# Feed-forward of a two-layer decoder in fp32r parts on one core: ten of eleven gate and up steps computed transposed, with the weights as stationary operand

## What is computed

```python
def rms_norm(x, g):
    y = xf * lax.rsqrt(jnp.mean(xf * xf, axis=-1, keepdims=True) + RMS_EPS)
    return (y * g.astype(jnp.float32)).astype(x.dtype)

def swiglu(x, w_gate_up, w_down):
    gate, up = jnp.split(x @ w_gate_up, 2, axis=-1)
    return (jax.nn.silu(gate) * up) @ w_down
...
        h = swiglu(rms_norm(x, g[2]), w_gate_up[layer], w_down[layer])
        x = x + rms_norm(h, g[3])
```

## Time and profile before

| | us |
|---|---|
| median of 3 runs | 799.78 |
| lowest, highest run | 798.93, 800.35 |
| profiled execution | 799.25 |
| its span | 797.5 |
| TensorE busy | 785.1 (98%) |
| VectorE busy | 503.6 (63%) |
| ScalarE busy | 382.7 (48%) |

### The profile page before, as it was taken

One profiled execution on the slowest core, in us unless ns is written; L12 is line 12 of the kernel. 1 busy time (PEld: TensorE's weight loads), 2 busy tenths in 40 slices (PEclk: granted clock), 3 DMA queues, 4 the chain that ended last, 5 costly groups with the idle time before them and its releaser, 6 DMA issues.

```text
span 797.5 us, 12942 instructions
## 1 busy us (share of the span) xinstructions
PE 785.1 (98%) x4795; PEld 689.8 (86%) x4795; DVE 503.6 (63%) x645; ACT 382.7 (48%) x469; POOL 59.4 (7%) x74
## 2 busy tenths in 40 slices
PE   8999999999999999998999999999999999999997
PEld 7999978888888888998999999999987888888885
DVE  5788987764655547776747557567546756555453
ACT  6675667443334335745545435445357433343331
POOL 1000002100000000311201202112002000000000
PEclk9999999999999999999999999999999999999999
DMA  8534665776455555287466455474722875555601
GB/s 230 172 114 132 218 191 171 238 254 219 160 173 195 181 191 162 52 219 205 111 180 170 126 165 152 140 196 125 245 80 73 275 273 164 171 197 179 222 21 53
DMA packets 158801, 135.45 MB, mean 170 GB/s; under 512 B 5176, under 2 KB 149168, under 8 KB 158768
## 3 DMA queue, kind: packets, MB, share of 16 engines
q1 hardware_dynamic: 157296, 130.75, 52.3%
q0 software_dynamic: 1376, 4.22, 2.4%
q10 hardware_dynamic: 96, 0.04, 0.0%
HBM read 133.91 MB, written 1.07 MB: 169 GB/s over the span
## 4 chain that ended last, share of the span: by engine, by line
PE 92%; ACT 3%; DVE 2%; DMA 1%; issue 1%; SPq 0%; DVEq 0%; POOLq 0%; ACTq 0%; POOL 0%
PE ps L1001 19%; PE ps L1003 19%; PE ps L1002 19%; PE ps L1007 8%; PE ps L1009 8%; PE ps L1008 8%; PE ps L1278 2%; PE ps L1268 2%; PE ps L1143 1%; PE ps L1247 1%; ACT xt L445 1%; DVE w_lo L642 1%; PE ps L1074 1%; PE ps L1241 1%; PE ps L1022 1%
## 5 line engine op out<-in xcount | busy, mean ns | idle before, releaser
L642 DVE TENSOR_TENSOR w_lo<-raw,w_hi 128x2048 fp32r<-128x2048 f32 (+2 forms) x146 | 280.4, 1941 | 35.8 <-ACT w_hi L414 34.3
L414 ACT ACTIVATE w_hi<-raw 128x2048 fp32r<-128x2048 f32 (+2 forms) x146 | 234.1, 1628 | 47.0 <-DMA raw<-in_w_kv_b 16.2
L1001 PE MATMUL ps<-w_hi,xt 128*128 128x512 f32 x352 | 139.4, 396 | 0.0
L1003 PE MATMUL ps<-w_hi,xt 128*128 128x512 f32 x352 | 137.3, 390 | 0.0
L1002 PE MATMUL ps<-w_lo,xt 128*128 128x512 f32 x352 | 137.1, 389 | 0.0
L537 ACT ACTIVATE work<-ps,stat 128x256 f32<-128x256 f32 x44 | 20.9, 476 | 199.9 <-PE ps L1003 199.9
L1007 PE MATMUL ps<-xt,w_hi 128*128 128x256 f32 x384 | 110.1, 287 | 1.1 <-DVE xt L650 0.7
L1008 PE MATMUL ps<-xt,w_hi 128*128 128x256 f32 x384 | 108.6, 283 | 0.0
L1009 PE MATMUL ps<-xt,w_lo 128*128 128x256 f32 x384 | 108.6, 283 | 0.0
L1001 PE MATMUL ps<-w_hi,ot 128*128 128x512 f32 x240 | 94.7, 395 | 0.0
L1003 PE MATMUL ps<-w_hi,ot 128*128 128x512 f32 x240 | 93.5, 390 | 0.0
(11 more groups left out here) (121 smaller groups left out, 1092.1 us busy)
## 6 DMA issues: line engine op xcount, KB each, us to landing
raw<-in_w_gate_up SPq DMA_DIRECT2D x88, 512.0 KB, 4.7
raw<-in_w_kv_b SPq DMA_DIRECT2D x96, 256.0 KB, 3.6
raw<-in_w_down SPq DMA_DIRECT2D x22, 1024.0 KB, 4.9
raw<-in_w_qkv_a SPq DMA_DIRECT2D x24, 512.0 KB, 4.8
raw<-in_w_q_b SPq DMA_DIRECT2D x48, 256.0 KB, 3.6
raw<-in_w_o_a SPq DMA_DIRECT2D x4, 1024.0 KB, 5.2
raw<-in_w_o_b SPq DMA_DIRECT2D x4, 1024.0 KB, 4.9
work<-in_norm_gains POOLq DMA_DIRECT2D x4, 512.0 KB, 5.2
```

What stands on the lines that cost most here:

```text
L414: act.activation(w_hi[:, s % CUT, 0:size(s)], raw[:, s % RAW, 0:size(s)], ACT.Copy).then_inc(hi_made, 1)
L642: dve.tensor_tensor(w_lo[:, c, 0:n], raw[:, s % RAW, 0:n], w_hi[:, c, 0:n].bitcast(F32), ALU.subtract).then_inc(lo_made, 1)
L1001: mm(out, xs[0], ws[0], start=start, stop=False)
L1003: return mm(out, xs[1], ws[0], start=False, stop=stop)
```

## The change

In steps 1 to 10 of each layer the gate and up products are made with the weights as stationary operand. A step has four of them: f (which 128 of the step's 256 hidden columns) and c (0 gate, 1 up), into bank 4 + 2f + c. For each of the eight row blocks a matmul takes the weights' high part as stationary operand and both parts of x, 256 + 256 tokens, as one moving row into the two halves of the bank; a second takes the low part and the high part of x (256 columns) into the first half. ScalarE copies the second half out, and VectorE adds it to the first. The result has hidden columns as partitions, so it needs no transpose; the norm's factors now lie along the free axis, so they are multiplied in from `rows`, once before the silu and once behind it. For that each layer's feed-forward part gets a diagonal, a spread into bank 7 and a copy of its own. Step 0 and the down products stay as they were, and step 0's hidden part is still transposed. The three loads, high parts and low parts per step remain.

The core of the diff (ScalarE, VectorE, TensorE). `up_part_of` and `gate_of` are like `gate_part_of`; `hidden_of` writes the high part into `ot`:

```diff
+            def gate_part_of(l, i, j, f):
+                n = wide_step(l, i)
+                act.wait_ge(cols_done, j * 6 + 3 * n + 2 * f + 1)
+                if n:
+                    act.wait_ge(gate_silu_made, j * 4 + 2 * n + f - 1)
+                act.activation(gate[:, f, :], bank(4 + 2 * f, SEQ, SEQ), ACT.Copy).then_inc(gate_part, 1)
+            def up_part_of(l, s, i, j, f):
+                n = wide_step(l, i)
+                act.wait_ge(*((cols_done, j * 6 + 3 * n + 2) if f == 0 else (w_used, j * 6 + s + 2)))
+                if n:
+                    act.wait_ge(hidden_made, j * 4 + 2 * n + f - 1)
+                act.activation(upper[:, f, :], bank(5 + 2 * f, SEQ, SEQ), ACT.Copy).then_inc(up_part, 1)
+            def gate_of(l, i, j, f):
+                n = wide_step(l, i)
+                act.wait_ge(gate_made, j * 4 + 2 * n + f + 1)
+                if n:
+                    act.wait_ge(hidden_made, j * 4 + 2 * n + f - 1)
+                act.activation(gate_silu[:, f, :], gate[:, f, :], ACT.Silu).then_inc(gate_silu_made, 1)
+            def hidden_of(l, i, j, f):
+                act.wait_ge(hidden_made, j * 4 + 2 * wide_step(l, i) + f + 1)
+                act.activation(ot[:, 0, hidden_at(i).start + f, :], hidden[:, f, :], ACT.Copy).then_inc(hidden_hi, 1)
             def swiglu_step(l, s0, i, j, units):
                 s = s0 + 3 * i - 1
-                for n, u in enumerate(units):
-                    if n < NT and i == 1:
-                        silu_of(l, s, i, j, n)
-                    hi(u, j)
-                    if n < NT and i > 1:
-                        silu_of(l, s, i, j, n)
+                if i > 1:
+                    up_part_of(l, s - 3, i - 1, j, 1)
+                hi(units[0], j)
+                if i > 1:
+                    hidden_of(l, i - 1, j, 1)
+                gate_part_of(l, i, j, 0)
+                gate_of(l, i, j, 0)
+                up_part_of(l, s, i, j, 0)
+                if len(units) > 1:
+                    hi(units[1], j)
+                hidden_of(l, i, j, 0)
+                if len(units) > 2:
+                    hi(units[2], j)
+                gate_part_of(l, i, j, 1)
+                gate_of(l, i, j, 1)
             def swiglu(l, s0, last_units):
                 for t in range(NT):
                     act.wait_ge(xrs_made, NT * (2 * l + 1) + t + 1)
-                    silu_of(l, s0, 0, 0, t)
+                    silu_of(l, s0, t)
                     if t == 0:
                         hi(s0 + 4)
                 swiglu_step(l, s0, 1, 0, range(s0 + 5, s0 + 8))
@@ -558,6 +601,8 @@
                     for i in (2, 3):
                         swiglu_step(l, s0, i, j, range(s0 + 3 * i + 2, s0 + 3 * i + 5))
                 swiglu_step(l, s0, STEPS - 1, 0, last_units)
+                up_part_of(l, s0 + 3 * STEPS - 4, STEPS - 1, 0, 1)
+                hidden_of(l, STEPS - 1, 0, 1)
...
+            def make_gate(l, i, j, f):
+                m = 2 * wide_step(l, i) + f + 1
+                dve.wait_ge(gate_part, j * 4 + m)
+                dve.tensor_tensor(gate[:, f, :], bank(4 + 2 * f, 0, SEQ), gate[:, f, :], ALU.add
+                                  ).then_inc(gate_summed, 1)
+                if i == 1 and f == 0:
+                    take_rows(2 + 2 * l, 7)
+                    cut_hidden(l)
+                dve.wait_ge(gate_summed, j * 4 + m)
+                dve.tensor_tensor(gate[:, f, :], gate[:, f, :], rows[:, :], ALU.mult).then_inc(gate_made, 1)
+            def make_hidden(l, i, j, f):
+                n = wide_step(l, i)
+                m = 2 * n + f + 1
+                dve.wait_ge(gate_silu_made, j * 4 + m)
+                dve.tensor_tensor(gate_silu[:, f, :], gate_silu[:, f, :], rows[:, :], ALU.mult).then_inc(gate_scaled, 1)
+                dve.wait_ge(up_part, j * 4 + m)
+                dve.tensor_tensor(upper[:, f, :], bank(5 + 2 * f, 0, SEQ), upper[:, f, :], ALU.add
+                                  ).then_inc(up_summed, 1)
+                dve.wait_ge(gate_scaled, j * 4 + m)
+                dve.wait_ge(up_summed, j * 4 + m)
+                if n:
+                    dve.wait_ge(hidden_cut, j * 4 + m - 2)
+                dve.tensor_tensor(hidden[:, f, :], upper[:, f, :], gate_silu[:, f, :], ALU.mult
+                                  ).then_inc(hidden_made, 1)
+            def lo_hidden(l, i, j, f):
+                k = hidden_at(i).start + f
+                dve.wait_ge(hidden_hi, j * 4 + 2 * wide_step(l, i) + f + 1)
+                dve.tensor_tensor(ot[:, 1, k, :], hidden[:, f, :], ot[:, 0, k, :].bitcast(F32), ALU.subtract
+                                  ).then_inc(hidden_cut, 1)
             def swiglu_step(l, i, j, units):
                 if i > 1:
-                    lo(units[0], j)
-                cut_hidden(l, i - 1, j)
-                gated(l, i, j, 0)
-                if i == 1:
-                    lo(units[0])
+                    make_hidden(l, i - 1, j, 1)
+                    lo_hidden(l, i - 1, j, 1)
+                make_gate(l, i, j, 0)
+                lo(units[0], j)
+                make_hidden(l, i, j, 0)
                 if len(units) > 1:
                     lo(units[1], j)
-                gated(l, i, j, 1)
+                lo_hidden(l, i, j, 0)
                 if len(units) > 2:
                     lo(units[2], j)
+                make_gate(l, i, j, 1)
             def swiglu(l, s0, last_units):
-                gated(l, 0, 0, 0)
+                gated(l, 0)
+                make_diagonal(2 * l + 1)
                 lo(s0 + 3)
-                gated(l, 0, 0, 1)
+                gated(l, 1)
                 lo(s0 + 4)
                 swiglu_step(l, 1, 0, range(s0 + 5, s0 + 8))
                 with dve.Fori(0, (STEPS - 3) // 2) as j:
                     for i in (2, 3):
                         swiglu_step(l, i, j, range(s0 + 3 * i + 2, s0 + 3 * i + 5))
                 swiglu_step(l, STEPS - 1, 0, last_units)
+                make_hidden(l, STEPS - 1, 0, 1)
+                lo_hidden(l, STEPS - 1, 0, 1)
...
+            def up_wide(l, s, i, j, f, c):
+                n, b = wide_step(l, i), 4 + 2 * f + c
+                if i == 1:
+                    if f == 0:
+                        pe.wait_ge(hid_made, 2 * l + c + 1)
+                    elif c == 0:
+                        pe.wait_ge(ht_made, l + 1)
+                    else:
+                        pe.wait_ge(rows_made, 2 + 2 * l)
+                else:
+                    pe.wait_ge(up_summed if c else gate_summed, j * 4 + 2 * n + f - 1)
+                both = bank(b).rearrange("p (n s) -> p n s", n=2)
+                for k in range(KT):
+                    if f == 0 and c == 0 and k % 4 == 0:
+                        pe.wait_ge(lo_made, j * 6 + s + k // 4 + 1)
+                    w_h, w_l = (v[:, k % 4, FC * c + P * f:FC * c + P * f + P] for v in cut_unit(s + k // 4, k=4))
+                    inst = mm(both, w_h, xt[:, :, k, :], start=k == 0, stop=k == KT - 1, skip_group_check=True)
+                    if f == 1 and c == 1 and k % 4 == 3:
+                        mm(bank(b, 0, SEQ), w_l, xt[:, 0, k, :], start=False, stop=k == KT - 1, skip_group_check=True
+                           ).then_inc(w_used, 1)
+                    else:
+                        inst = mm(bank(b, 0, SEQ), w_l, xt[:, 0, k, :], start=False, stop=k == KT - 1,
+                                  skip_group_check=True)
+                if f == 0 or c == 0:
+                    inst.then_inc(cols_done, 1)
...
+                if i == 0:
+                    pe.wait_ge(ht_made, l + 1)
+                else:
+                    pe.wait_ge(hidden_cut, j * 4 + 2 * wide_step(l, i) + 2)
...
                 s = s0 + 3 * last - 1
-                up(l, s, last, 0, 0)
-                transpose_hidden(l, last - 1, 0)
-                up(l, s, last, 0, 1)
-                down_part(l, s + 2, last - 1, 0, 0, FH[:2])
-                transpose_hidden(l, last, 0)
-                down_part(l, s + 2, last - 1, 0, 0, FH[2:])
+                for f, c in FH:
+                    up_wide(l, s, last, 0, f, c)
+                down_part(l, s + 2, last - 1, 0, 0, FH)
...
-                up(l, s, i, j, 0)
-                transpose_hidden(l, i - 1, j)
-                up(l, s, i, j, 1)
+                up_wide(l, s, i, j, 0, 0)
+                if i == 1:
+                    spread_rows(2 + 2 * l, 7)
+                    transpose_hidden(l)
+                up_wide(l, s, i, j, 0, 1)
+                up_wide(l, s, i, j, 1, 0)
+                up_wide(l, s, i, j, 1, 1)
```

More of the change, by code:

```diff
@@ L167, in build @@
         hid = carve(NT * FC).rearrange("p (t n) -> p t n", t=NT)
+        gate, gate_silu, upper, hidden = (carve(2 * SEQ).rearrange("p (f n) -> p f n", f=2) for _ in range(4))
         qb = carve(NG * SEQ, 0).rearrange("p (g n) -> p g n", g=NG)
@@ L234, in build @@
             "up0_done", "silu_made", "hid_made", "ht_done", "ht_hi", "ht_made"))
```

(31 more changed lines are left out.)

44 lines of the change are left out of this document (12 added, 32 removed).

## The result

The changed kernel takes **813.49 us** (median of 4 runs, 812.81 to 815.36), the kernel before 799.57 us beside it (798.93 to 800.35): ratio 1.0181, 95% interval [1.0167, 1.0196], slower by 1.8%. The forecast was 808.4 with a range to 813.0, so the direction is right, and the size is 5 us short and just outside the range. The profiled execution has a span of 811.1 us, 13.6 more than before.

A forecast was written before the change was run, and what follows sets the result against it. TensorE was taken to bound the kernel (785.1 us of a 797.5 span, 92% of the chain). TensorE's own work -4.2, waits +10.0 and clock +3.4 gave +9.2 on 799.25: 808.4 us, range 802.5 to 813.0.

The forecast's parts named there:

- The first wide step: Step 1 of each layer: TensorE waits for the second gate unit's cut and for bank 6, +10.0 us over both layers.
- The long wait: Step 1 of each layer: TensorE waits for bank 6 behind ScalarE's copy held by a DMA, 4.2 and 3.0 us.
- the links behind the landing: Step 1: high part, gate copy, gate sum, rows and two hidden cuts in a single chain, 4.65 us in all.
- The clock: After each layer's long wait the granted clock falls to half, losing 1.7 us each, +3.4; bounds 0 and twice that.
- TensorE's own work: TensorE's stream: transposes -9.4, gate and up pairs +4.3, two spreads of the norm's factors +0.9, together -4.2 us.
- The gain from the transposes: Feed-forward steps: each layer keeps one of 11 groups of hidden transposes, 20 x 0.47 = -9.4 us.
- is a mixed stream just the sum?: Gate and up pairs: asked whether mixing 512 and 256 columns costs extra; answered with nothing added, a pair 0.3467 us.
- six matmuls: Attention's two matmuls of 512 and four of 256 columns took 0.94 us against 0.93 from the two prices.
- The bound that I named: Gate and up pairs: if every 256-column matmul were as costly as a 512, 3.4 us more per step.
- Cover in the steady steps: Steady feed-forward steps: ScalarE's 9.5 and VectorE's 11.9 us fit into 16.5, so no TensorE wait, 0 added.
- The early transfer: Rival, first wide steps: second half lands at T+4.65 and T+3.85 (T the step's start), clock kept, 800.0 us; chance 0.10.
- Only TensorE's work: Rival: the change does only its TensorE work, with none of the waits, 795.0 us; chance 0.03.

The follow-up runs named there:

- edit 1: Changed kernel, but in step 1 of each layer ScalarE copies the first gate product ahead of the next unit's high part: 803.99 us, ratio 1.0068.
- edit 7: Changed kernel with edit 1 and edit 2 together: 802.20 us, ratio 1.0042.
- edit 5: Changed kernel without the product of the weights' low part with x's high part in the wide steps: 747.85 us in one run.
- edit 8: As edit 7, and in steps 2 to 10 all 32 wide products before the 32 narrow ones: 807.09 us, ratio 1.0103.
- second profile of the kernel before: The kernel before, unchanged, profiled once more: at attention it waited 2.37 us and lost nothing of the clock.
- edit 3: Changed kernel with xt laid out so that both parts of x are one stretch: 812.81 us, ratio 1.0173.
- edit 6: Changed kernel with the narrow product added into the other half of the bank: 815.52 us in one run.
- edit 2: Changed kernel, but VectorE makes the diagonal behind the cut of the second gate unit: 816.09 us, ratio 1.0214.

## Why the prediction was right or wrong

**The first wide step: right in mechanism, 2 us high in size.** The diagonal waited for GpSimd and TensorE for the cut behind it: 1.27 and 1.28, predicted 1.4. The long wait stood where it was put, ScalarE's copy released by a DMA and TensorE by the second cut of step 0's hidden part: 2.84 and 2.62, predicted 4.2 and 3.0. All waits: 8.0 us instead of the +10.0. Counted from the start of step 1, the landing came at T+6.5 and T+6.3 (predicted 7.66 and 6.49 less 0.3: 7.4 and 6.2); TensorE reached bank 6 not at T+6.4 but, its first wait taken off, at T+6.9 in both layers; and the links behind the landing took 4.5, predicted 4.65 (as listed they add up to 4.6). From issue to landing this transfer took 6.0 to 7.5 us in the twelve profiles, so the wait can't be known better than to about 1 us. Edits 1 and 7 show the mechanism: with the order on the two queues changed, there is no such wait.

**The clock: half right.** I put 1.7 us on each long wait. Layer 1's had it: clock 0.55, 0.50, 0.50 and 0.74 of full speed from 637 to 641. Layer 0's, a longer one, had none. Slices of the changed kernel there:

```profile
152.00:153.00 1.00, 0.00 (x0) 0.00 (x0) 0.93 (x3) 0.00 (x0) 0.00 (x0) 1.00 1.02 406
153.00:154.00 1.00, 0.40 (x2) 0.35 (x3) 1.00 (x3) 0.09 (x1) 0.00 (x0) 1.00 0.60 238
154.00:155.00 1.00, 1.00 (x8) 0.87 (x7) 1.00 (x1) 1.00 (x3) 0.00 (x0) 1.00 0.07 20
```

So +1.7 in this profile instead of the +3.4.

**TensorE's own work: the step that failed.** The prediction put the price of mixing widths at nothing ("So I add nothing for the mixture or the strided read"). "TensorE's own work: -9.4 + 4.3 + 0.9 = -4.2" came out as +1.4 (the 13.6 less 8.0 of waits, 1.7 of clock in layer 1, 2.2 at attention and 0.3 at the start), 5.6 off. In steps 2 to 9 it should have been 16 x -0.26 = -4.2 and was 0.0. The mis-sized term is the pair: 0.353 and not 0.3467, 0.20 us per step, 4.0 over 20 steps; and 0.06 per step in the down products behind them, 1.2. The rest is 0.4. The gain from the transposes was sized rightly; what edits 5 and 8 add up to (7.25, 3.83, 5.44 to 5.47) is the step that I forecast, 16.5.

The error was in how I answered "is a mixed stream just the sum?". I took six matmuls at 0.94 us against a computed 0.93 as proof that nothing was to be added. But those six are two wide ones and then four narrow ones: one return to wide products, not one for each wide product as in the pairs. And a reading to 0.01 us can't tell a surplus of 0.006 per pair from none, while 640 pairs make 4 us of it. The trace's exact starts show both: the six take 0.933 us, the plain sum, but the two wide ones 0.234 and 0.235 and the four narrow ones 0.116 on average, so the surplus was there and was cancelled in this row. The bound that I named (3.4 us per step) didn't help either: it was so far off that I set it aside, and took 0.

**Luck.** Against the profiled 812.81 us the forecast is 4.4 low: TensorE's own work +5.6, attention +2.2, the start +0.3, less 2.0 for the waits and 1.7 for the clock. That two terms were too high hid nearly half of the miss; had they come as forecast, the time would have been 816.5.

The weighing against the Trainium skill (TensorE: Matmul & The Clock Gate, Back-to-back issue gap) was settled by the earlier trace rows, and rightly: edit 5's 0.2266 for a wide product and edit 8's 0.1198 for a narrow one are again about 13 ns over N / 2.4. Its gap would have put the result lower still, at 804.9. That section gives the formula for an isolated matmul; for streams with weight loads it names 131 ns at 512 columns, which is further still from the 0.2267 us here.

**Cover in the steady steps: right.** No wait in steps 2 to 10, so "nothing for these" held. The slack was real but not as free as it looked: edit 8 spent it at the end of each layer and paid 5.8 us.

**Attention: not foreseen.** 2.2 us lie where nothing was changed. 1.1 of it is the clock (3.42 lost after the wait in place of 1.71, with 0.5 of it while TensorE stood idle), which differs from run to run of one kernel, as the second profile of the kernel before with no loss shows. But the medians differ by 13.9, the profiles by 13.6, so the other runs have something of this size too; whether it is in the same place no run here shows.

**The rivals.** The early transfer needed a landing at T+4.65 or earlier; it was at T+6.5. The 3.2 us that the prediction took from the Trainium skill (DMA: Bandwidth & Descriptors, Anatomy of one DMA) come from a fit given there for DMAs issued by GpSimd; these loads are SyncE's and took 6.0 to 7.5 us (and with 3.2 us the prediction's own terms give 798.5, not 798.4). "Only TensorE's work", 795.0, falls twice: on the waits, and with edit 7 at 802.2 on its own sum.

## What to carry to other kernels

A price per instruction from a uniform stream isn't the price in a mixed one: multiply the smallest difference that a reading can hide by how often it will occur before setting it to zero, and take the reading from the order that the new kernel will have. Where operands of two widths meet on TensorE, group equal widths, but look at which result the next engine wants first, since the grouping that was cheapest for TensorE here delivered all results late. And in an in-order queue an operation that waits for a transfer belongs behind those whose inputs are ready: one operation moved on ScalarE took 5.5 us of waits off TensorE here, and with clock and attention 9 us off the time, while removing the smaller wait ahead of the long one gained nothing.

## What the runs showed of the hardware

- **Wide products behind narrow ones take longer, and the narrow ones a little less.** In the trace's starts, as means over eight steps: in pairs 0.236 and 0.117 us, where either width by itself takes 0.2267 and 0.1200. Gate and up of one step take 11.29 us with 32 returns to wide products (edits 3 and 6 too), 11.20 with 8, 11.09 with 1. What in the engine causes it stays open; separate stretches, the half of the bank and the other engines' traffic it isn't.
- **The effect outlasts the narrow products.** The 24 down products behind them take 5.50 us (pairs), 5.49 (groups of four) or 5.47 (32 and 32), and 5.44 without narrow ones; the excess is in the first ten. The kernel before shows the same behind its transposes of 128 columns: from 249.26 to 250.87 seven wide products took 0.230 each.
- **The clock's fall doesn't follow the length of a wait alone.** After waits of 2.2 to 4.7 us the profiles show a loss of 1.71 us, of twice that, or none: none after 2.84 (changed kernel, 153.6) and 2.37 (kernel before, second profile); 1.71 after 2.22 (kernel before), 2.62 (changed kernel) and even 3.73 (edit 3, layer 0); 3.42 after 3.35 in the changed kernel's attention and after 4.70 with edit 2. In the slices of the changed kernel it begins inside the wait, and lasts:

```profile
367.00:368.00 1.00, 0.00 (x0) 0.00 (x0) 1.00 (x2) 1.00 (x3) 0.68 (x1) 0.72 0.06 18
368.00:369.00 1.00, 0.52 (x3) 0.52 (x4) 0.96 (x4) 1.00 (x1) 0.56 (x1) 0.50 0.00 0
...
374.00:375.00 1.00, 1.00 (x9) 1.00 (x8) 1.00 (x1) 0.00 (x0) 0.00 (x0) 0.86 0.95 265
```

- **One transfer's time to landing varies by 1.5 us with the same queue ahead of it.** The second half of unit s0 + 5 in layer 0 took 7.2 and 6.5 us in two profiles of the kernel before, 6.0 in the changed kernel, 7.5 with edit 7: as much as several of the terms that a forecast like this argues about.
